# Two layers in split float32: three 256-column matmuls per weight tile in place of one of 512 and one of 256

## The reference, cut to what matters

```python
# first layer
p = rms_norm(x, pre_mix_norm) @ w_in          # 2048 x 5640 in tiles of 128, then four mixers
x = x + rms_norm(y @ w_out, post_mix_norm)
hid = causal_dwconv(rms_norm(x, pre_ffn_norm) @ ffn_up, conv_w, conv_b)     # 2048 x 11264
x = x + rms_norm((gelu(gate) * val) @ ffn_down, post_ffn_norm)              # 5632 x 2048
# second layer
x = x + 0.5 * swiglu(rms_norm_2(x), w_gate, w_up, w_down)                   # 2 x (2048 x 5632), 5632 x 2048
proj = rms_norm_2(x) @ w_in_2                                               # heads, values, gates
x = x + (sigmoid(g_dil) * (o_dil @ w_dil) + sigmoid(g_diff) * (o_diff @ w_diff)) @ w_out_2
x = x + 0.5 * swiglu(rms_norm_2(x), ...)
```

## Time and profile before

| | |
|---|---|
| Time, median of 3 runs | 3714.75 us (3706.88 to 3719.52) |
| Span of the profiled execution, first to last instruction | 3704.6 us |
| Mean granted TensorE clock | 0.966 of full |
| PE matmul | 3483.8 us busy, 94%, 19548 instructions |
| PE weight load | 3021.9 us, 82% |
| DVE | 2257.1 us, 61% |
| ACT | 1736.4 us, 47% |
| POOL | 594.1 us, 16% |
| DMA | 615.77 MB, 166 GB/s on average |

### The profile page before, as it was taken

The page is one execution under the profiler, slowest core; times in us unless marked ns, Lnnn a source line. Parts: engine busy times, 40 slices in busy tenths (PEclk is TensorE's granted clock), DMA queues, the critical chain, the costliest instruction groups (busy, mean ns, idle before and its releaser), DMA issues. The chain is left out here.

```text
span 3704.6 us, 60346 instructions
## 1 busy us (share of the span) xinstructions
PE 3483.8 (94%) x19548; PEld 3021.9 (82%) x19548; DVE 2257.1 (61%) x2911; ACT 1736.4 (47%) x2556; POOL 594.1 (16%) x580
## 2 busy tenths in 40 slices
PE   8996678999999989999999988899989999999999
PEld 7886567888888878888888877788877888888887
DVE  6557257777774465565555577755557655555444
ACT  4442245555554454454544444444446544444343
POOL 0110202111110021111100056631100111111000
PEclk9996689999999999999999999999989999999999
DMA  5550034555555645555556644455445555555565
GB/s 196 187 186 10 6 101 139 188 190 190 188 180 176 189 142 193 191 186 190 191 173 188 200 150 139 136 187 168 156 134 173 170 188 186 182 187 185 172 188 166
DMA packets 173846, 615.77 MB, mean 166 GB/s; under 512 B 20544, under 2 KB 20704, under 8 KB 173280
## 3 DMA queue, kind: packets, MB, share of 16 engines
q1 hardware_dynamic: 173648, 614.04, 51.5%
q10 hardware_dynamic: 144, 1.05, 0.1%
HBM read 610.81 MB, written 4.19 MB: 166 GB/s over the span
## 5 line engine op out<-in xcount | busy, mean ns | idle before, releaser
L298 PE MATMUL acc<-moving_halves,weights_high 128*128 128x512 f32 x6848 | 2441.4, 400 | 36.3 <-DVE moving_halves L479 21.0
L249 DVE TENSOR_TENSOR weights_low<-weights_raw,weights_high 128x1024 fp32r<-128x1024 f32 (+1 forms) x1184 | 1461.1, 1245 | 852.3 <-ACT weights_high L242 851.6
L300 PE MATMUL acc<-moving_halves,weights_low 128*128 128x256 f32 x6848 | 1926.7, 281 | 0.0
L242 ACT ACTIVATE weights_high<-weights_raw 128x1024 fp32r<-128x1024 f32 (+1 forms) x1184 | 1221.0, 1033 | 856.8 <-PE acc L300 841.2
L298 PEld LDWEIGHTS acc<-moving_halves,weights_high 128*128 128x128 f32 x6848 | 1293.2, 189 | 353.7 <-issue 40.5
L300 PEld LDWEIGHTS acc<-moving_halves,weights_low 128*128 128x128 f32 x6848 | 1302.9, 190 | 6.9 <-issue 5.6
L298 PE MATMUL acc<-gated_halves,weights_high 128*128 128x512 f32 x2112 | 737.9, 394 | 17.1 <-PEq L898 10.3
L300 PE MATMUL acc<-gated_halves,weights_low 128*128 128x256 f32 x2112 | 591.5, 280 | 0.0
L334 ACT ACTIVATE cross_products<-acc 128x256 f32<-128x256 f32 x512 | 196.3, 383 | 693.8 <-PE acc L300 693.8
L298 PEld LDWEIGHTS acc<-gated_halves,weights_high 128*128 128x128 f32 x2112 | 397.9, 188 | 107.3 <-issue 18.0
L357 POOL TENSOR_TENSOR ffn_hidden<-unscaled,token_scale 128x256 f32<-128x256 f32 x264 | 219.2, 830 | 1257.6 <-DVE unscaled L340 790.6
(11 more groups left out here) (300 smaller groups left out, 1605.0 us busy)
## 6 DMA issues: line engine op xcount, KB each, us to landing
weights_raw<-in_w_in SPq DMA_DIRECT2D x272, 512.0 KB, 4.1
weights_raw<-in_ffn_up SPq DMA_DIRECT2D x176, 512.0 KB, 4.3
weights_raw<-in_ffn_w_gate SPq DMA_DIRECT2D x176, 512.0 KB, 4.1
weights_raw<-in_ffn_w_up SPq DMA_DIRECT2D x176, 512.0 KB, 4.6
weights_raw<-in_ffn_w_down SPq DMA_DIRECT2D x160, 512.0 KB, 3.8
weights_raw<-in_ffn_down SPq DMA_DIRECT2D x80, 512.0 KB, 4.0
weights_raw<-in_w_out SPq DMA_DIRECT2D x64, 512.0 KB, 4.1
weights_raw<-in_ffn_w_down SPq DMA_DIRECT2D x32, 256.0 KB, 2.6
```

The lines of the kernel that those rows point to most:

```text
L242: core.nc.scalar.activation(core.high[:, slot, 0:nk, :].rearrange("p a b -> p (a b)"), core.raw[:, slot, 0:nk * P], ACT.Copy).then_inc(cor ...
L249: core.nc.vector.tensor_tensor(core.low[:, slot, 0:nk, :].rearrange("p a b -> p (a b)"), core.raw[:, slot, 0:nk * P], core.high[:, slot, 0 ...
L298: core.nc.tensor.matmul(acc[:, bank, :, :], core.high[:, u % SLOTS, k, :], x, start=(k0 + k == 0), stop=False)
L300: last = core.nc.tensor.matmul(acc[:, bank, 0, :], core.low[:, u % SLOTS, k, :], x[:, 0, :], start=False, stop=(k0 + k == nk_all - 1))
```

## The change

Each weight tile now gets three matmuls of 256 columns, all into half 0 of the bank: low weights with the high part of the operand, high weights with the low part, high weights with the high part. Half 1 of the bank is no longer written. `take_cross` returns at once: ACT copies nothing. `take_tile` on DVE waits for `slots_free` of the tile's last chunk itself (as ACT did) and copies half 0 to the output in place of the addition. The sum of the three products is the same, in another order of additions.

```diff
--- before.py
+++ after.py
@@ -295,9 +295,10 @@
             if before is not None:
                 before(t, prod.first[t] + k0 + k)
             x = parts[:, prod.first[t] + k0 + k, :, :]
-            core.nc.tensor.matmul(acc[:, bank, :, :], core.high[:, u % SLOTS, k, :], x,
+            core.nc.tensor.matmul(acc[:, bank, 0, :], core.low[:, u % SLOTS, k, :], x[:, 0, :],
                                   start=(k0 + k == 0), stop=False)
-            last = core.nc.tensor.matmul(acc[:, bank, 0, :], core.low[:, u % SLOTS, k, :], x[:, 0, :],
+            core.nc.tensor.matmul(acc[:, bank, 0, :], core.high[:, u % SLOTS, k, :], x[:, 1, :], start=False, stop=False)
+            last = core.nc.tensor.matmul(acc[:, bank, 0, :], core.high[:, u % SLOTS, k, :], x[:, 0, :],
                                          start=False, stop=(k0 + k == nk_all - 1))
         last.then_inc(core.slots_free, 1)
 
@@ -328,16 +329,14 @@
 
 def take_cross(core, act, prod, acc, i, t):
 
+    return
+
+
+def take_tile(core, dve, prod, acc, out, i, t):
+
     last = prod.of_tile(t)[-1][0]
-
-    act.wait_ge(core.slots_free, i * prod.per_body + (SLOTS + core.chunk + last + 1))
-    core.nc.scalar.activation(core.cross[:, t % 2, :], acc[:, t % 2, 1, :], ACT.Copy).then_inc(core.cross_ready, 1)
-
-
-def take_tile(core, dve, prod, acc, out, i, t):
-
-    dve.wait_ge(core.cross_ready, i * len(prod.tiles) + (core.tile + t + 1))
-    core.nc.vector.tensor_tensor(out, acc[:, t % 2, 0, :], core.cross[:, t % 2, :], ALU.add).then_inc(core.acc_free, 1)
+    dve.wait_ge(core.slots_free, i * prod.per_body + (SLOTS + core.chunk + last + 1))
+    core.nc.vector.tensor_copy(out, acc[:, t % 2, 0, :]).then_inc(core.acc_free, 1)
 
 
 def taken(core, eng, prod, i, t):
```

## The result

The changed kernel takes 3770.18 us (median of 4 runs, 3768.5 to 3770.51); the kernel before took 3710.82 in the runs beside it (3706.2 to 3719.52). The ratio is 1.0147, with a 95% interval of 1.0126 to 1.0168. It is slower by 59 us. I had forecast 3706, a small gain; the result lies inside the range and on the side of the rival "each load and start costs", to which I gave 0.32.

The account below looks back on a forecast made before the run. It took PE's matmul cadence, pairs times start-to-start time, as the bound outside a few places. Matmuls +7.3, heads -12.0, ends -3.8 gave -8.5 us on a 3704.6 span; plus 10.2 to the median, 3706 us, range 3625 to 3790.

Parts of the forecast that it names:

- each load and start costs: Slower rival, matmuls: 13.4 ns excess per matmul whatever its columns, a triple of 360 ns, 3792 us; chance 0.32.
- I take 116.8 because it is the same instruction with the same load behind it: Matmul step: each 256-column matmul keeps the narrow one's 116.8 ns interval, so three take 350 ns a weight tile.
- 0.442 ns a column and 3.6 ns a matmul: Check on the matmul price: line through 230 ns (512 columns) and 116.8 (256); one more matmul adds about 3.5 ns.
- 26.8 ns over two matmuls: Slower rival's basis: a pair's excess over 2.4 GHz, 346.8 - 320, 13.4 ns for each matmul; chance 0.32.
- the excess splits 17 to 10: Argument against the slower rival: the pair's excess divides between wide and narrow matmul more like the columns than evenly.
- It decides from 117.0 ns an interval on: Threshold for the slower rival: at a triple of 351.0 ns the matmul cadence takes back the 15.8 us gained elsewhere.
- Two kinds of stages: Steady stages: 4928 pairs at 346.7 ns and 2816 at 353.2, assigned to particular products; after the change 350 in both.
- The rival's 370 for the second kind: Slower rival in the 353.2 ns stages: excess there is 33 ns a pair, so a triple would take 370 ns.
- I take the same distance: Last step from profiled span to median time: the changed kernel's median also lies 10.2 us above its span.
- The rival's 3792: Slower rival's total: triples of 360 ns throughout, 93 us more, less 15.8 us gained elsewhere; chance 0.32.
- The head bodies: 20 bodies of the second input product: DVE copies before ACT's root ends, 0.60 us saved a body, 12.0 us.
- Ends, ACT, DVE, order: Nine stage ends save 0.42 us each, 3.8 us; ACT's and DVE's saved time hidden in steady stretches; accumulation order costs nothing.

Follow-up runs that it names:

- low_wide: Kernel before with the low-weight matmul widened to 512 columns, adding the fourth product, so two wide matmuls a tile: 4610.31 us (one run).
- split_only: Kernel before with its wide matmul cut into two of 256 columns, both halves, ACT copy and DVE addition kept: 3797.52 us, ratio 1.0219.
- grouped: Kernel before with each chunk's matmuls reordered, eight wide ones and then eight narrow ones: 3711.34 us, ratio 0.9984.
- before_again: Kernel before, unchanged, profiled once more: 3707.86 us (one run).
- act_early: Kernel before with ACT's copy of the second tile's half 1 moved ahead of put-back and root in the head bodies: 3694.69 us, ratio 0.9951.
- bf16_three: Changed kernel with its three matmuls reading the upper 16 bits of the operands as bfloat16: 3601.84 us (one run).
- uneven: Kernel before with its wide matmul cut into 384 and 128 columns, the 256-column one kept: 4190.91 us (one run).
- snake_early: Kernel before with chunks ordered wide, narrow, narrow, wide, plus ACT's earlier copy in the head bodies: 3688.53 us, ratio 0.993.

## Why the prediction was right or wrong

**The matmuls: wrong, and this decided the sign.** The step that failed is "I take 116.8 because it is the same instruction with the same load behind it", and with it the line that gave 0.442 ns a column and 3.6 ns a matmul. In a stream of alternating widths the starts are shifted: the records show 230 and 116.8 where the streams of one width show 226.7 and 120.0 (low_wide, split_only), and in grouped the narrow starts are 113 and 119 ns only right behind a change of width. Only the sum, 346.7, is a cost; its division by the starts isn't. A shift of 3.3 ns turned a price of 13.3 ns a matmul into one of 3.6, and a triple of 360.0 ns into one of 350. The right reading stood among the rivals, 26.8 ns over two matmuls, and I argued it down with "the excess splits 17 to 10", the same shifted starts. "It decides from 117.0 ns an interval on" was right: the interval is 120.0.

The rule of the Trainium skill ("TensorE: Matmul & The Clock Gate", "Back-to-back issue gap"), a fixed 2.5 ns for every warm matmul whatever its columns, has the shape that the runs confirm at 256 and 512 columns. The section gives it for isolated matmuls, and not for a stream of loads and matmuls as this one; the prediction left that condition out. The trace does not agree with its size: 13.3 ns here for float32r with a load for each matmul, 6.7 for bfloat16.

**Two kinds of stages: half right.** I expected the triple to be the same in both, and it is 360.0 in all. But I took the 353.2 as a property of places. It is not (before_again): the 6.7 ns more appear in streams of alternating widths alone, and the kernels with matmuls of one width show none. In the products that happened to be at 346.7 the change costs 13.3 ns a tile, in those at 353.3 it costs 6.7. The rival's 370 for the second kind never came.

**From span to median.** "I take the same distance", 10.2 us, was wrong for the same reason. Some 2 us lie between span and time in every execution (3768.4 and 3770.51 in the profiled one of the changed kernel); the other 8 were luck, since the profiled execution before was a fast draw of a kernel that spreads over 35 us. The changed kernel does not spread, and its median lies 1.8 us above its span.

**The rival's 3792** was 22 us too high: 8.4 from that distance, 7.2 from the heads, 3.6 from the matmuls (93 against 89.4), and the rest from the gaps between products and the end, 1.8 more than the 3.8 that I counted, and from the first matmul, 0.85 us earlier.

**The head bodies: mechanism right, size too small.** I said 0.60 us a body, 12.0 in all; it is 1.02 us in the body shown, and 19.2 in all. The start of L1990 behind the root moved as I said. What I left out is the next step: before, DVE's L1992 began beside POOL's scaling of the tile and took 1.12 us; now the tile is scaled earlier and the same instruction, L1991, takes 0.69. The mean by lines, kernel before and then after:

```profile
L1992 DVE SCALAR_TENSOR_TENSOR x_T<-x_T 128x512 f32<-128x512 f32 x19 | 21.2, 1116 | 0.7
```

```profile
L1991 DVE SCALAR_TENSOR_TENSOR x_T<-x_T 128x512 f32<-128x512 f32 x19 | 13.2, 692 | 0.6
```

That is the other 0.42 us. The overlap with POOL is what goes with it in every trace. In act_early, where only ACT's order was changed, 19 of the 20 begin after POOL is done and take 0.69; the first still begins inside POOL's instruction:

```profile
2166.23 1.00 POOL L357 TENSOR_TENSOR arena<-unscaled,token_scale 128x256 f32 x1 [6.43 <-DVE unscaled L340]
2166.67 1.11 DVE L1994 SCALAR_TENSOR_TENSOR x_T<-x_T 128x512 f32<-128x512 f32 x1
```

It is not the overlap as such: before, L1990 was under way when POOL's instruction began at 2223.66, ran 0.40 us beside it, and took 0.68 all the same. As I said, the heads cover the matmuls' price: PE still waits in them, 21.0 us where it waited 37.2.

**Ends, ACT, DVE, order: right.** The ends from an up to a down product and from down 1 to the second input product gained 0.38 to 0.43 us each, and so did the end of the program; the gaps ahead of the branches and of up 2 gained 1.8 and 1.0. The copy on DVE takes 423 ns for the 420 that I took, ACT's saved time shows nowhere outside the heads and ends, and three additions into one half cost nothing (split_only against the changed kernel).

**The chances.** 116.8 was the likeliest by my own reading, but the interval in which the answer was "same" was 0.8 ns wide, and the reading shown was good to 3 ns at best. Of the price of a matmul start, which 9216 instructions would multiply, I had one equation with two unknowns. With the column's price set to the clock that the rows grant (2.4 GHz) there is one unknown left, and the answer is 13.4 ns; that deserved more than 0.32.

## What to carry to other kernels

Before splitting a matmul, price the start: take the period of a repeating pattern, subtract the columns at the granted clock, and divide by the number of matmuls; never read a price from a single start-to-start distance in a stream of mixed widths. Of the two widths measured the wide matmul is the cheaper way to use a loaded weight tile (226.7 ns for 512 columns, 240.0 in two of 256), and removing work from ACT or DVE pays only where PE waits for them, which here a changed order of two instructions did as well. A kernel whose runs spread by 1% may hold a state that alternates; one profile is then one draw, and its distance to the median can't be carried over.

## What the runs showed of the hardware that was not expected

- In a stream of one width, a float32r matmul that loads its own 128 x 128 weights costs its columns at 2.4 GHz plus 13.3 ns, at 256 columns (120.0, split_only) and at 512 (226.7, low_wide). In bfloat16 the 256-column one costs 113.3, with a load record of 96 ns in place of 193 (bf16_three).
- With 384 + 128 + 256 columns a tile takes 406.7 ns, 46.7 over that law (uneven); a floor of some 113 ns under each load would explain it, and so might the changes of width.
- A stream that alternates 512 and 256 columns runs at 346.7 or at 353.3 ns a pair, and which one changes from execution to execution of the same kernel and from product to product within one (five profiles). Groups of eight take 349.2 and groups of sixteen 347.9, the same in every product (grouped, snake_early): 20 ns for a change to wide and one back.
- DVE's three-operand instruction on 512 elements took 1.11 to 1.12 us when it began inside a POOL instruction and 0.69 without. One that had begun before POOL's took its usual 0.68.
